# Stick-breaking scores in a two-block transformer kernel: one fp32 product replaced by three products of rounded parts

## The reference, cut to what matters

```
qa = rms_norm(split_heads(q_sb, 8), sb_q_gain)      # 8 heads, 512 tokens, 128 wide
ka = rms_norm(split_heads(k_sb, 8), sb_k_gain)
z = einsum('bhqd,bhsd->bhqs', qa, ka) / sqrt(128)   # the scores
past = key_pos < q_pos
log_not = where(past, log_sigmoid(-z), 0)
later = reverse_cumsum(log_not) - log_not
w = where(past, exp(log_sigmoid(z) + later), 0)
oa = (w @ v) * silu(z_sb)
```

## Time and profile before

| | |
|---|---|
| median of 3 runs | 2550.31 us |
| profiled execution, its own time | 2548.95 us |
| its span, first to last instruction | 2547.2 us |
| mean granted clock of TensorE | 0.991 of full speed |
| PE busy | 2503.2 us, 98% |
| DVE busy | 1624.5 us, 64% |
| ACT busy | 973.7 us, 38% |
| POOL busy | 105.2 us, 4% |
| DMA | 390.58 MB, mean 153 GB/s |
| between 1600 and 2050 us (stick-breaking heads) | PE 449.43 of 450 us busy |

### The profile page before, as it was taken

One profiled execution on the slowest core, in us unless ns is written; L12 is line 12 of the kernel. 1 busy time (PEld: TensorE's weight loads), 2 busy tenths in 40 slices (PEclk: granted clock), 3 DMA queues, 4 the chain that ended last, 5 costly groups with the idle time before them and its releaser, 6 DMA issues.

```text
span 2547.2 us, 30034 instructions
## 1 busy us (share of the span) xinstructions
PE 2503.2 (98%) x11939; PEld 2015.9 (79%) x11939; DVE 1624.5 (64%) x2448; ACT 973.7 (38%) x1549; POOL 105.2 (4%) x113
## 2 busy tenths in 40 slices
PE   7999999999999999999999999999999999999999
PEld 4789777777778877888888887888888787887787
DVE  4456776677776768776776768456465577656532
ACT  4232444434454333432334333445455432333421
POOL 0000000000000113000000113000000000000000
PEclk8999999999999999999999999999999999999999
DMA  9955433334434754666655754323232245532342
GB/s 349 333 193 182 132 108 116 124 125 132 133 100 153 250 167 160 204 199 210 197 163 174 248 174 151 114 78 90 76 91 83 75 151 168 175 111 90 124 151 83
DMA packets 293133, 390.58 MB, mean 153 GB/s; under 512 B 11698, under 2 KB 221234, under 8 KB 289154
## 3 DMA queue, kind: packets, MB, share of 16 engines
q1 hardware_dynamic: 287184, 355.84, 43.9%
q0 software_dynamic: 5808, 32.84, 3.4%
q10 hardware_dynamic: 2, 0.00, 0.0%
HBM read 371.85 MB, written 16.78 MB: 153 GB/s over the span
## 4 chain that ended last, share of the span: by engine, by line
PE 90%; DVE 4%; ACT 2%; DMA 2%; issue 1%; SPq 1%; DVEq 0%; ACTq 0%
PE G L2147 75%; PE OB L2147 6%; PE S L2147 6%; PE TB L2150 2%; PE TB L2147 1%; DMA MORE<-in_ev_mod_w 1%; DMA MRAW<-in_ev_mod_w 1%; DVE MACC L1630 1%; DVE WLO L1624 1%; DVE TT L1624 1%; ACT PB L1435 1%; DVE SM L1852 0%; SPq L1128 0%; PE OB L2150 0%; DMA LATE<-in_ev_mod_w 0%
## 5 line engine op out<-in xcount | busy, mean ns | idle before, releaser
L2147 PE MATMUL G<-HHI,WLO 128*128 128x512 f32 x2560 | 1005.6, 393 | 0.0
L2147 PE MATMUL G<-HHI,WHI 128*128 128x512 f32 x1928 | 793.0, 411 | 5.8 <-issue 3.3
L2147 PE MATMUL G<-HLO,WHI 128*128 128x512 f32 x1928 | 755.2, 392 | 0.0
L2147 PEld LDWEIGHTS G<-HHI,WLO 128*128 128x128 f32 x2560 | 482.2, 188 | 107.8
L1262 ACT ACTIVATE WHI<-RAW 128x1024 fp32r<-128x1024 f32 x282 | 297.4, 1055 | 563.2 <-PE G L2147 502.1
L1624 DVE TENSOR_TENSOR WLO<-RAW,WHI 128x1024 fp32r<-128x1024 f32 x282 | 344.5, 1223 | 239.4 <-ACT WHI L1262 237.6
L2147 PEld LDWEIGHTS G<-HHI,WHI 128*128 128x128 f32 x1928 | 364.0, 189 | 86.1 <-issue 10.7
L2147 PEld LDWEIGHTS G<-HLO,WHI 128*128 128x128 f32 x1928 | 364.3, 189 | 78.3 <-issue 6.7
L1630 DVE SCALAR_TENSOR_TENSOR MACC<-MWIDE,SC,MACC 128x512 f32<-128x512 f32 x420 | 320.4, 763 | 40.1 <-DMA MWIDE<-in_w_ada 12.4
L2147 PE MATMUL G<-HHI,WHITA 128*128 128x512 f32 x536 | 217.9, 406 | 0.0
L2147 PE MATMUL G<-HLO,WHITA 128*128 128x512 f32 x536 | 210.9, 394 | 0.0
(11 more groups left out here) (347 smaller groups left out, 3055.9 us busy)
## 6 DMA issues: line engine op xcount, KB each, us to landing
RAW<-in_w_in SPq DMA_DIRECT2D x128, 512.0 KB, 3.7
MWIDE<-in_od_mod_w SPq DMA_DIRECT2D x96, 512.0 KB, 4.3
MWIDE<-in_w_ada SPq DMA_DIRECT2D x96, 512.0 KB, 4.7
RAW<-in_ev_w_in SPq DMA_DIRECT2D x80, 512.0 KB, 3.6
RAW<-in_od_w_in SPq DMA_DIRECT2D x64, 512.0 KB, 3.9
MWIDE<-in_ev_mod_w SPq DMA_DIRECT2D x32, 512.0 KB, 4.0
RAW<-in_ev_w_out SPq DMA_DIRECT2D x32, 512.0 KB, 3.5
RAW<-in_od_w_out SPq DMA_DIRECT2D x32, 512.0 KB, 3.5
```

The source lines that it names most:

```text
L2147: return e.o.matmul(o, l, r, start=start, stop=stop, skip_group_check=True)
```

## The change

For each of the 16 keys a stage `z_split` is put into the plan, one step behind `nr_apply`, at the point where the next key begins and ahead of its `nr_square`. In it ACT waits for the normed tile (`v_nr`, "end") and copies it, rounded, to `Q2HI` or `K2HI`; DVE waits for that copy and subtracts it from the tile, and writes the low part in place of the tile (`Q2LO`, `K2LO` share the memory of `Q2`, `K2`). The high parts have two slots each, in tiles 8 to 11 of `Y`, which are free until the silu of gate tile 8; that silu gets a wait for the last scores. `st_z` on PE then does three fp32r products in place of one fp32 product, and waits for the low part. No `yield` is added, so all stages of before keep their places. The retention heads (`rt_z`) are as they were.

```diff
@@ make_plan, sb_task
                     put("nr_apply", key)
                     yield
+                    put("z_split", key)
@@ act_program
+            elif stage == "z_split":
+                key, = a
+                what, h = key
+                e.wait_ge(v_nr, (key, "end"))
+                if h > 1:
+                    e.wait_ge(p_z, (h - 2, 0))
+                else:
+                    e.wait_ge(spill, 3)
+                    e.wait_ge(v_tile, (3, KT - 1))
+                cp((Q2HI if what == "q3" else K2HI)[:, h % 2, :], rows_of(key)[0]).then_inc(*a_ev.up((key, "high")))
@@ dve_program
+            elif stage == "z_split":
+                key, = a
+                what, h = key
+                hi, lo = (Q2HI, Q2LO) if what == "q3" else (K2HI, K2LO)
+                e.wait_ge(a_ev, (key, "high"))
+                tt(lo[h // 2 % 2][:, h % 2, :], rows_of(key)[0], f(hi[:, h % 2, :]), SUB).then_inc(
+                    *v_nr.up((key, "z low")))
@@ dve_program, silu_b
+                if layer == 3 and k >= 8:
+                    e.wait_ge(p_z, (7, 0))
@@ pe_program
-                e.wait_ge(v_nr, (("k3", h), "end"))
-                mm(z_bank(kt), K2[b][:, i, c0:c0 + P], Q2[b][:, i, c0:SEQ], True, True).then_inc(*p_z.up((h, kt)))
+                if stage == "rt_z":
+                    e.wait_ge(v_nr, (("k3", h), "end"))
+                    mm(z_bank(kt), K2[b][:, i, c0:c0 + P], Q2[b][:, i, c0:SEQ], True, True).then_inc(*p_z.up((h, kt)))
+                else:
+                    kh, kl = K2HI[:, i, c0:c0 + P], K2LO[b][:, i, c0:c0 + P]
+                    qh, ql = Q2HI[:, i, c0:SEQ], Q2LO[b][:, i, c0:SEQ]
+                    e.wait_ge(v_nr, (("k3", h), "z low"))
+                    mm(z_bank(kt), kh, qh, True, False)
+                    mm(z_bank(kt), kh, ql, False, False)
+                    mm(z_bank(kt), kl, qh, False, True).then_inc(*p_z.up((h, kt)))
```

More of the change, by code:

```diff
@@ L186, in build @@
     QLO = scratch("QLO", [P, 2, SEQ], F32R, 42 * K1)
+    Q2LO = [scratch(f"Q2LO{i}", [P, 2, SEQ], F32R, i * 4 * K1) for i in range(2)]
+    K2LO = [scratch(f"K2LO{i}", [P, 2, SEQ], F32R, 8 * K1 + i * 4 * K1) for i in range(2)]
+    Q2HI, _ = place("Q2HI", [P, 2, SEQ], F32R, y0 + 16 * K1)
+    K2HI, _ = place("K2HI", [P, 2, SEQ], F32R, y0 + 20 * K1)
     LS2 = [LS, LSB]
```

## The result

The changed kernel takes 2558.99 us, the median of five runs (2556.5 to 2564.79), against 2550.95 us for the kernel before in the same comparison (2549.54 to 2553.23). The ratio is 1.0034, with a 95% interval of 1.0023 to 1.0045: slower, by about 8 us. The profiled execution took 2556.5 us, with a span of 2554.7 us and a mean granted clock of 0.992.

What follows compares the result with a forecast made beforehand. PE, busy 2503.2 of 2547.2 us, was taken to bound the kernel. Products at -3.2 and waits at +11.0 gave +7.8, 2556.8 us; the median 1.4 above the profiled run made it 2558, range 2552 to 2563.

Steps and rivals of the forecast that it cites:

- The waits: PE in the stick-breaking heads waits for late SQLO and V copies: 10.15 us plus 0.9 of restarts, 11.0 in all.
- k0, k1, q5: Norms where a weight split stands between SQHI and SQLO: SQLO comes 2.05 later and PE waits 1.2 us each.
- V copy: ACT's V copies, queued behind k1's copy waiting for its norm, make PE restart 2.75 us late; largest single wait.
- k3: Silu and a split at k2 push q3's refinement, its own copy on top: PE waits 0.95 at k3's sum.
- At k6: Delay handed on through silu and a split, as at k2, giving a PE wait of 0.65 us.
- q1, k4, first cumulative sum of head 4: Edges where SQLO at two norms, and late DVE and ACT work at the sum, miss PE by 0.1 each.
- restarts: After each late SQLO, PE's next product starts 0.34 later, not 0.23: about eight at 0.11, 0.9 us.
- The products: Three fp32r products for one fp32 score save PE about 0.4 us a head, 3.2 for eight heads; ends 2.2 and 3.8.
- What costs nothing: Waits for last scores, spill and tile 15, high slots, st_z's low part and late weight splits cost PE nothing.
- Only the products count: Rival: ACT and DVE have slack, no wait arises, and time falls by 3.2 to 2547.1 us; chance 0.08.
- Half the waits: Rival: the V wait stays, key waits mostly fit gaps, about 5.5 us in all, 2552.6 us; chance 0.2.
- The clock falls: Rival: PE's clock halves after the two or three longest waits, costing 2 us each more, 2563 us; chance 0.07.

Runs made afterwards that it cites:

- the version without them: All sixteen splits kept but placed later (three behind the next key's nr_low, the fourth behind the first scores), against the changed kernel: 2549.96 us, ratio 0.9990 to the kernel before.
- scores in fp32: Changed kernel with its splits in place but one fp32 product per score, low parts written to an unread tile: 2561.7 us, ratio 1.0039 to the kernel before.
- two copies for one: Changed kernel with each split's tile first copied on ACT to an unread tile of Y: 2565.96 us, ratio 1.0058 to the kernel before.

## Why the prediction was right, point by point

**The waits.** They were put at 11.0 us; the changed kernel's stretch is 10.50 us longer than the version without them. The lateness of each, as the distance of starts less the ordinary 0.23:

| wait at | forecast, us | measured, us |
|---|---|---|
| k0, k1, q5 | 1.2 each | 1.16, 1.07, 1.04 |
| V copy | 2.75 | 2.73 |
| k5 | 1.9 | 1.79 |
| k3 | 0.95 | 0.66 |
| q7 (in the forecast: "At k6") | 0.65 | 0.75 |
| q1, k4, first cumulative sum of head 4 | 0.1 each | 0.00, 0.00, 0.00 |
| restarts | 0.9 | 0.96 (nine) |

The seven waits add up to 9.20 us and the restarts to 0.96; the last 0.3 lies in distances behind the waits that are wider by up to 0.02 each. At q1 and k4 `SQLO` came just in time, and PE paid the restart all the same.

The chain worked out for q0 to k0 stands in the trace with its steps: copy 0.03 behind the norm's end (0.09 forecast), square 0.54 behind the copy, `SQHI` 0.65 behind the square. The forecast of k3 went over several handed-on delays, and there it was off the most, by 0.3.

**The products.** This term was mis-sized: 3.2 us forecast, with ends of 2.2 and 3.8, and 2.11 measured in the version without waits. The mechanism holds. The step that failed is the price of narrow products. From two products of 128 columns in 0.17 I took 0.25 for three, and named 0.33 only as an end; it is 0.34, since three products and the one behind them start about 0.11 apart after the first (1697.60, 1697.71, 1697.82), and the product behind starts its successor late too. At 256 columns it was 0.40 and not 0.36. The forecast also rounded up: its own 2.22 - 1.84 makes 0.38 a head and 3.1 in all. The Trainium skill ("FP8 and Floating Point Precision", TensorE Precision Notes) gives true FP32 four passes, from which the forecast had an estimate of 4.3 us. Here the measurement decides, at half of that.

**What costs nothing** held: no wait on the scores, on `Y`, on the silu of the later gate tiles, or on weight splits is in the trace of the changed kernel. One wait that was there before was passed over in the reading of the stretch, the 0.57 for a copy of K at 1999.26, ahead of the retention heads; it is 0.71 or 0.72 in every version with three products and 0.57 in those with one.

**The rivals.** "Only the products count" did not happen, and is what the later splits bring about. "Half the waits" did not happen; the seven larger waits worked out from the plan are all there, and the three edges of 0.1 left at most a restart. "The clock falls" was a rival at 0.07 and is in part real: not in the changed kernel's own profile, but in two of the experiments' profiles behind waits of 2.2 to 3.1 us, at 1.4 to 1.6 us each, where the forecast had 2. The five runs of the changed kernel go the same way: the two slowest, 2561.94 and 2564.79 us, have mean granted clocks of 0.990 and 0.988, the fastest, 2556.5, has 0.992. That the spread of the runs is this clock was not tested.

**Net.** The forecast was + 7.8 for a profiled execution. The stretch, which holds all the splits and the changed scores, grew by 8.39, so the forecast was 0.6 too low: the saving was sized 1.1 too large and the waits 0.5 too large, and about half of the one error hides the other. That the span's 7.5 is nearer is luck, since PE reached q0 0.9 earlier in this execution. For the median 2558 was forecast and 2558.99 measured; it lies 2.5 above the profiled execution, where 1.4 was assumed.

## What to carry to other kernels

Ask of every instruction added to an in-order engine what it waits for and what stands behind it, before asking how long it takes. Sixteen copies of 0.63 us on an engine that is idle for 60% of the span cost 10 us, because they stood at the head of the queue while their input was still being made, and at nine places PE had no slack for it; moved behind work that was ready, the same copies cost nothing. The length counts too where the slack is gone: a second copy cost about another 0.5 us or more at each of the nine. And price a replacement of a slow product by fast ones at its narrowest shape: here three fp32r products of 128 columns took 0.34 us and the one fp32 product 0.23.

## What the runs showed of the hardware that was not expected

Behind a PE wait of the same length and place (2.53 to 2.58 us idle, for the V copy) the granted clock fell to 0.5 in one of five kernels' profiled executions (scores in fp32, 2.53) and stayed at 1.00 in the other four. Where it fell it lasted about 3 us and cost 1.4 us, half of the wait again. With two copies for one it fell behind both 3.08 and 2.17 us. What decides it stays open. The Trainium skill ("TensorE: Matmul & The Clock Gate", Part 1) holds that throttling is the default and activity releases it. These traces agree with the direction: in this stretch the clock fell only behind waits of over 2 us, and came back to 1.00 while PE was busy (1676 to 1678 us above).

Even at the full clock a wait has a tail: the first product after a wait for `SQLO` starts its successor 0.34 later and not 0.23 (1642.84 to 1643.17 in the changed kernel, as in the earlier trace rows), after 0.5 us of idle as after 1.6; after the V wait it is 0.31. A product pays this even without idle, if what it waits for comes at the last moment. At q1 in the changed kernel (DVE, then PE):

```profile
1650.82 0.69 DVE L1639 TENSOR_TENSOR SQLO<-SQ,SQHI 128x512 fp32r<-128x512 f32 x1 [0.49 <-ACT SQHI L1267]
...
1651.58 0.49 PE L2171 MATMUL TB<-SQHI,ONER 128*128 128x512 f32 x1
1651.91 0.39 PE L2171 MATMUL TB<-SQLO,ONER 128*128 128x512 f32 x1
```

`SQLO` ends at 1651.51, 0.07 before PE starts on time; the successor still starts 0.33 later. In the kernel before, it started 0.22 later at this sum (1651.19 to 1651.41).
